# Feed-forward products on unnormed x: the inverse norm moves behind the matmuls

## The reference

```python
def rms_norm(x, w, eps=NORM_EPS):
    y = x32 * lax.rsqrt(jnp.mean(x32 * x32, axis=-1, keepdims=True) + eps)
    return (y * w.astype(F32)).astype(x.dtype)

def swiglu(x, w_gate, w_up, w_down):
    return (jax.nn.silu(x @ w_gate) * (x @ w_up)) @ w_down
# per layer:
x = x + 0.5 * swiglu(rms_norm(x, ffn1_norm), ...)      # hidden width 2816
x = x + hybrid_mixer(rms_norm(x, mix_norm), ...)
x = x + 0.5 * swiglu(rms_norm(x, ffn2_norm), ...)
```

## Time and profile before

| | |
|---|---|
| median of 3 runs | 1400.5 us (1397.87 to 1402.68) |
| the profiled execution | 1402.49 us |
| its span, first to last instruction | 1400.6 us |
| granted TensorE clock, mean | 0.985 |
| TensorE busy | 1348.2 us, 96% |
| VectorE busy | 925.3 us, 66% |
| ScalarE busy | 652.9 us, 47% |
| GpSimd busy | 350.9 us, 25% |

### The profile page before, as it was taken

One profiled execution on the slowest core, in us unless ns is written; L12 is line 12 of the kernel. 1 busy time (PEld: TensorE's weight loads), 2 busy tenths in 40 slices (PEclk: granted clock), 3 DMA queues, 4 the chain that ended last, 5 costly groups with the idle time before them and its releaser, 6 DMA issues.

```text
span 1400.6 us, 26198 instructions
## 1 busy us (share of the span) xinstructions
PE 1348.2 (96%) x11102; PEld 1312.7 (94%) x11102; DVE 925.3 (66%) x1323; ACT 652.9 (47%) x942; POOL 350.9 (25%) x235
## 2 busy tenths in 40 slices
PE   6999999999999999999999999998999999999998
PEld 6999999889898999999999999998888989999997
DVE  6777556876976865555477774567678677655554
ACT  6444547542234454444454454566322343544442
POOL 2000015445742720000210000244368245200000
PEclk9999999989999999999999999999899999999999
DMA  6565654533232646556556556464333335555553
GB/s 226 190 189 194 195 176 138 156 114 107 75 105 77 181 143 189 187 192 218 178 161 181 184 186 199 139 179 139 106 91 90 94 119 166 165 181 187 191 177 123
DMA packets 61316, 220.17 MB, mean 157 GB/s; under 512 B 6928, under 2 KB 7184, under 8 KB 60688
## 3 DMA queue, kind: packets, MB, share of 16 engines
q1 hardware_dynamic: 61200, 218.50, 49.6%
HBM read 217.42 MB, written 1.05 MB: 156 GB/s over the span
## 4 chain that ended last, share of the span: by engine, by line
PE 76%; DVE 16%; ACT 4%; issue 2%; DMA 1%; POOL 1%; SPq 0%; DVEq 0%; ACTq 0%
PE bank L480 23%; PE bank L481 22%; PE bank L482 22%; DVE wlo L1236 2%; PE bank L729 2%; DVE qkv L1451 2%; ACT whi L891 1%; PE bank L500 1%; DVE bank L1574 1%; DVE tmpA L1573 1%; DVE flat L1256 1%; PE bank L717 1%; DMA raw<-weights 1%; POOL wlo L1145 1%; DVE tmpA L1466 1%
## 5 line engine op out<-in xcount | busy, mean ns | idle before, releaser
L480 PE MATMUL bank<-xh,whi 128*128 128x256 f32 x2384 | 679.2, 285 | 7.0 <-DVE wlo L1236 3.0
L481 PE MATMUL bank<-xl,whi 128*128 128x256 f32 x2384 | 671.0, 281 | 0.0
L482 PE MATMUL bank<-xh,wlo 128*128 128x256 f32 x2384 | 669.5, 281 | 0.0
L1236 DVE TENSOR_TENSOR wlo<-raw,whi 128x1024 fp32r<-128x1024 f32 (+1 forms) x346 | 437.3, 1291 | 158.1 <-ACT whi L891 156.1
L480 PEld LDWEIGHTS bank<-xh,whi 128*128 128x128 f32 x2384 | 453.5, 190 | 16.4 <-issue 7.0
L891 ACT ACTIVATE whi<-raw 128x1024 fp32r<-128x1024 f32 (+1 forms) x414 | 417.7, 1035 | 99.4 <-DMA raw<-weights 78.6
L481 PEld LDWEIGHTS bank<-xl,whi 128*128 128x128 f32 x2384 | 453.5, 190 | 0.3
L482 PEld LDWEIGHTS bank<-xh,wlo 128*128 128x128 f32 x2384 | 453.1, 190 | 0.0
L1145 POOL TENSOR_TENSOR wlo<-raw,whi 128x1024 fp32r<-128x1024 f32 x68 | 172.4, 2542 | 204.2 <-ACT whi L891 204.2
L1186 POOL TENSOR_TENSOR flat<-flat 128x256 f32<-128x256 f32 x36 | 33.6, 933 | 716.3 <-ACT flat L910 715.3
L480 PE MATMUL bank<-hh,whi 128*128 128x256 f32 x704 | 196.9, 280 | 0.0
(11 more groups left out here) (347 smaller groups left out, 1409.6 us busy)
## 6 DMA issues: line engine op xcount, KB each, us to landing
raw<-weights SPq DMA_DIRECT2D x350, 512.0 KB, 3.8
raw<-weights SPq DMA_DIRECT2D x64, 448.0 KB, 4.0
cst<-consts SPq DMA_DIRECT2D x1, 1088.0 KB, 11.7
par<-params SPq DMA_DIRECT2D x1, 1072.5 KB, 7.9
par<-params SPq DMA_DIRECT2D x1, 1060.5 KB, 9.6
x<-x_in SPq DMA_DIRECT2D x1, 1024.0 KB, 6.1
y_out<-ret SPq DMA_DIRECT2D x4, 256.0 KB, 2.2
ropec<-positions SPq DMA_DIRECT2D x1, 128.0 KB, 2.1
```

What stands on the lines that cost most here:

```text
L480: mm(out, w[0], a[0], start=start, stop=False)
L481: mm(out, w[0], a[1], start=False, stop=False)
L482: return mm(out, w[1], a[0], start=False, stop=stop)
L1236: V.tensor_tensor(slot(wlo, i), slot(raw, i), r32(slot(whi, i)), ALU.subtract).then_inc(S("low_dve"), 1)
```

## The change

- For both feed-forward steps `xh` and `xl` are made from x times the norm weights, without the inverse norm: `high_scaled` on ScalarE and `low_scaled` on VectorE (all eight tiles; GpSimd makes none). At FFN2 and at FFN1 of layer 1 this is done tile by tile as the stage before hands x over.
- The sums of squares, and the matmuls that spread the inverse norm, now stand between the products of units 0 and 1 (`late_sums` before tile 4 of the gate halves, `late_inverse` before the first up half; in layer 0 `column_sums` and `late_inverse` within the up halves). Their `keep_busy` matmuls go. ScalarE copies the inverse norm to SBUF (`copy_inverse`).
- For every unit VectorE multiplies the gate by the inverse norm out of PSUM into `tmpB`, and ScalarE takes the SiLU from there. `up` runs one unit behind for the product with up and two for `hl`. In `down` of a feed-forward step there are two linked VectorE instructions: PSUM times factor times inverse norm, then the addition to x.
- At the start the first two weight pieces are transferred ahead of x, which comes in two halves; the large part of the parameters goes behind piece 7 and the large part of the constants behind piece 12. TensorE runs 24 `keep_busy` matmuls.
- The rotary remainders move from before layer 0 to between the last table step and `down` of layer 0. Units 0 and 1 now run before the S5 parameters, and table steps start with unit 11, so that the last two stand behind the last unit.
- The merged branches get `mgh` and `mgl` of their own, since `xh` and `xl` are filled while the output projection runs. The mixer's norm stays as it was. Of the feed-forward pieces `gu1_0.0` goes from GpSimd to VectorE.

```diff
         def sync_first(sp):
-            sp.dma_start(ropec.bitcast(mybir.dt.int32), positions).then_inc(once["small_loads"], 16)
             sp.dma_start(cst[:, 0:EARLY], consts[:, 0:EARLY]).then_inc(once["small_loads"], 16)
-            sp.dma_start(x, x_in).then_inc(once["x_load"], 16)
+            sp.dma_start(slot(raw, 0), weight_piece(0)).then_inc(once["raw0"], 16)
             sp.dma_start(par[:, 0:NORMS], layer_params(0)[:, 0:NORMS]).then_inc(S("norms"), 16)
-            for i in range(RAW_SLOTS):
-                sp.dma_start(slot(raw, i), weight_piece(i)).then_inc(once[f"raw{i}"], 16)
-            sp.dma_start(par[:, NORMS:], layer_params(0)[:, NORMS:]).then_inc(S("par"), 16)
-            sp.dma_start(cst[:, EARLY:], consts[:, EARLY:]).then_inc(once["tables_load"], 16)
+            sp.dma_start(slot(raw, 1), weight_piece(1)).then_inc(once["raw1"], 16)
+            sp.dma_start(x[:, 0:4, :], x_in[:, 0:4, :]).then_inc(once["x_load"], 16)
+            sp.dma_start(x[:, 4:8, :], x_in[:, 4:8, :]).then_inc(once["x_load2"], 16)
+            sp.dma_start(slot(raw, 2), weight_piece(2)).then_inc(once["raw2"], 16)
+            sp.dma_start(ropec.bitcast(mybir.dt.int32), positions).then_inc(once["position_load"], 16)
...
+                if i == 7:
+                    sp.dma_start(par[:, NORMS:], layer_params(0)[:, NORMS:]).then_inc(S("par"), 16)
...
+            def late_sums(which):
+
+                sum_of_first(which)
+                pe.wait_ge(*since("squares", 5 * which + 5))
+                for j in range(2):
+                    last = mm(sum_banks[j][:, 0:1], squared[:, KD - 1, j * P:(j + 1) * P], one_col, start=False, stop=True)
...
+                if f == 2:
+                    first_two(units, scaled, 0, early={4: lambda: late_sums(1)}, mid={0: lambda: late_inverse(2)})
...
+                    first_two(units, scaled, 0, mid={4: column_sums}, late={2: lambda: late_inverse(1)})
...
+            def high_scaled(wname, ks):
+
+                for k in ks:
+                    A(xh[:, k, :], x[:, k, :], ACT.Identity, scale=par_(wname, k, k + 1)).then_inc(S("xh"), 1)
...
-                    act.wait_ge(S("main"), main.ready(f"gu{f}_{m}"))
-                    if m >= 2:
-                        act.wait_ge(S("main_dve"), main.taken(f"gu{f}_{m - 2}"))
-                    A(tmpB[:, m % 2, :], main.bank(f"gu{f}_{m}")[:, 0:SEQ], ACT.Silu).then_inc(S(f"silu{f}"), 1)
+                    act.wait_ge(*since("gated", MF * (f - 1) + m + 1))
+                    A(tmpB[:, m % 2, :], tmpB[:, m % 2, :], ACT.Silu).then_inc(S(f"silu{f}"), 1)
...
+            copy_inverse(1)
+            silus(1, range(0, 2))
             act.wait_ge(S("par"), 16)
...
+                    if m == 0:
+                        dve.wait_ge(*since("inv_copied", f))
+                    dve.wait_ge(S("main"), main.ready(f"gu{f}_{m}"))
+                    V.tensor_tensor(tmpB[:, m % 2, :], main.bank(f"gu{f}_{m}")[:, 0:SEQ], invb, ALU.mult).then_inc(S("gated"), 1)
+                    if m:
+                        hidden(f, m - 1)
                     if m >= 2:
...
+                        low_hidden(f, m - 2)
...
+                            link(V.scalar_tensor_tensor(ps, ps, scale, over(invb, n), ALU.mult, ALU.mult))
+                            V.tensor_tensor(x[:, tiles, :], x[:, tiles, :], ps, ALU.add).then_inc(S("main_dve"), 1)
+                        if low and (done := tiles.start):
+                            low(range(done - (1 if done == 7 else 2), done))
...
+            up(1, [0, 1])
...
-            for m in range(9, MF):
+            for m in range(11, MF):
                 up(1, [m])
-                turn_tables(m - 9)
+                turn_tables(m - 11)
+            turn_tables(11)
+            if not Now.layer:
+                rope_turns()
             down("dn1_", 0.5)
```

More of the change, by code:

```diff
@@ L276, in trunk @@
         small = sb("small", 176)
+        invb = two("invb", 1)[:, 0, :]
+        mgh, mgl = (two(f"mg{part}", KD, dt=F32R, over="big", skip=8 * SEQ * i) for i, part in ((1, "h"), (2, "l")))
         ropec, ropes = two("ropec", 1)[:, 0, :], two("ropes", 1)[:, 0, :]
@@ L529, in half @@
                 wh, wl = piece(f"{unit}.{o}")
+                if unit.startswith("wo"):
+                    high, low = mgh, mgl
+                else:
+                    high, low = xh, xl
                 for k in range(KD):
-                    last = product(ps, (wh[:, k, :], wl[:, k, :]), (xh[:, k, :], xl[:, k, :]), k == 0, k == KD - 1)
+                    if k in at:
+                        at[k]()
+                    last = product(ps, (wh[:, k, :], wl[:, k, :]), (high[:, k, :], low[:, k, :]), k == 0, k == KD - 1)
                 last.then_inc(S("main" if PIECES[PIECE_INDEX[f"{unit}.{o}"]][2] else "part"), 1)
@@ L537, in pair, with column_sums, late_inverse, norm_tile @@
                 half(unit, 1)
-            def norm_tile(which, k):
-                return since("normed_pool" if k % 2 else "normed_dve", which * KD // 2 + k // 2 + 1)
-            def first_two(units, arrived, wait, bank=4):
+            def column_sums():
+                pe.wait_ge(once["squares_added"], 1)
+                for j in range(2):
+                    for k in range(4):
+                        last = mm(sum_banks[j][:, 0:1], squared[:, k, j * P:(j + 1) * P], one_col, start=(k == 0), stop=(k == 3))
+                last.then_inc(once["sums_in"], 1)
+            def late_sums(which):
+                sum_of_first(which)
+                pe.wait_ge(*since("squares", 5 * which + 5))
+                for j in range(2):
+                    last = mm(sum_banks[j][:, 0:1], squared[:, KD - 1, j * P:(j + 1) * P], one_col, start=False, stop=True)
+                last.then_inc(S("sums"), 1)
+            def late_inverse(f):
+                if f == 2:
+                    pe.wait_ge(*since("inv_rms", 2))
+                elif Now.layer:
+                    pe.wait_ge(*since("inv_rms", 0))
+                else:
+                    pe.wait_ge(once["inv_in"], 1)
+                for j in range(2):
+                    last = mm(inv_bank[:, j * P:(j + 1) * P], inv_rms[:, j:j + 1].to_broadcast([P, P]), ident, start=True, stop=True)
+                last.then_inc(once["inverse"], 1)
+            def norm_tile(k):
+                return since("normed_pool" if k % 2 else "normed_dve", k // 2 + 1)
+            def first_two(units, arrived, wait, bank=4, early={}, mid={}, late={}):
+                high, low = (mgh, mgl) if units[0] == "wo0" else (xh, xl)
                 banks = [main_bank(u) for u in units]
@@ L1292, in down @@
                         dve.wait_ge(S("main"), main.ready(unit))
[L1293 to L1301 removed]
+                        ps = halves(main.bank(unit)[:, 0:n * SEQ], n)
@@ L1303, in vector_layer @@
+            if not Now.layer:
+                split_to(2)
+                dve.wait_ge(S("norms"), 16)
+                dve.wait_ge(once["x_load"], 16)
+                dve.wait_ge(once["x_load2"], 16)
+                dve.wait_ge(once["small_loads"], 16)
+                low_scaled(1, "n1", range(KD))
+                split_to(4)
+                dve.wait_ge(once["rms_in"], 1)
+                V.reciprocal(inv_rms, rms_col).then_inc(once["inv_in"], 1)
+            up(1, [0, 1])
             lre, lim = par_("lre"), par_("lim")
```

262 lines of the change are left out of this document (136 added, 126 removed).

## The result

The changed kernel takes 1406.42 us in the median of 18 runs (1398.15 to 1411.23), the kernel before 1400.2 us (18 runs, 1397.72 to 1404.71). The ratio is 1.0048 with a 95% interval of 1.0035 to 1.006: slower by about 6.7 us by the ratio. Predicted were 1405.3 us and a range of 1395 to 1412. The profiled execution took 1408.41 us, span 1406.6, mean granted clock 0.979; before it was 1402.49, 1400.6 and 0.985.

The account below looks back on a forecast made before the run. TensorE, busy for all but 0.3 us of some 187 us in each feed-forward stage, was taken as the bound. Terms -9.45 +1.45 +0.95 +5.25 -0.3 +5.55 -5.7 -0.95 +1.35 +3.4 +3.3 = +4.85 gave 1405.3 us, range 1395 to 1412.

Parts of the forecast that it names:

- The start: Before the first product: it comes at 10.2 us instead of 19.65, 9.45 us earlier (9.0 to 10.5).
- Norm products: Units 0 and 1 of layer 0: TensorE pays for column sums (0.9) and inverse (0.55) between products, +1.45 us.
- Parameters: Layer 0, before piece 6: parameters queued behind piece 7 land at 30.5 us, piece ready 34.7, wanted 29.45; +5.25 us.
- The clock: Half clock after waits: +3.4 us for layer 0's two long stalls, +3.3 for two of four gaps of about 2 us.
- The second feed-forward part: Edge from output projection to FFN2: products start 4.25 us earlier, less 0.85 and 0.55; -2.85 us each, -5.7 for both.
- Layer 1's first feed-forward part: FFN1 of layer 1: products start 5.0 us earlier, partly given back by sums, inverse and a late piece 6; net -0.95 us.
- Units inside a stage: Steady units: VectorE's extra product of 0.42 us is covered by idle time, 0; units over 5.65 us would refute the prediction.
- Rival 5: VectorE becomes the bound of each unit: 1420 us or more; chance 0.03.
- rival 3: Splits are further ahead than read, so neither long stall of layer 0 arises: 1391 us, clearly faster; chance 0.14.
- rival 1: Parameters land by 28 us, the stall is 2.7 us without a clock fall: 1401.1 us, no change; chance 0.16.
- Rival 2: No gap lowers the clock: -6.7 us, 1398.6 us, still no change; chance 0.13.
- rival 4: All gaps lower the clock and the parameters take 7.9 us: 1411 us; chance 0.12.

Follow-up runs that it names:

- the early transfer: Changed kernel with the large parameter transfer issued at the very start, behind the positions, rather than behind weight piece 7; ratio 1.0037 to the kernel before.
- putting the pieces first: Changed kernel with weight pieces 6 and 7 split on ScalarE and VectorE ahead of the wait for the parameters; ratio 1.0006 to the kernel before.
- The spread chain: Changed kernel with the nine groups of rotary remainders run one behind each of the last nine units of layer 0's first feed-forward part; ratio 1.0009 to the kernel before.
- the filled waits: Changed kernel with 16 and 22 small products on constants ahead of the two long-stalled products, layer 0 only; ratio 1.001 to the kernel before.
- The second edge experiment: Changed kernel with both first pieces of the second feed-forward part split ahead of the third output-projection unit's scaled copies and square; ratio 1.0009 to the kernel before.
- the first edge experiment: Changed kernel with each output-projection weight piece split one piece earlier on ScalarE and VectorE, ahead of the scaled copies of x; ratio 1.0053 to the kernel before.
- the last kernel: Changed kernel with spread rotary steps, pieces ahead of parameters, both edge pieces split earlier, parameters issued early, ninth piece split between small-step groups; 1386.02 us, ratio 0.9906.

## Why the prediction came out as it did

The forecast (1405.3) is 1.1 us from the median, its sign and its mechanism were right: large gains at the edges, given back by low weight parts that come late in the order of VectorE's and ScalarE's queues. But several terms were off and cancelled, so that it came this close is in part luck.

**The start.** -8.84 for -9.45. I had x landed at 9.7; ScalarE began to scale its first half at 8.84, but VectorE, whose program waits for both halves, made the first low part at 10.19, and the first product followed 0.62 later. In the other executions with this start the first product was at 11.02 to 11.74, so this one was early.

**Norm products.** +1.45 predicted. The column sums took 1.70 us from the first of them to the next product (17.89 to 19.59) rather than 0.9, the inverse 0.36 rather than 0.55. The row that I costed them from gives records, and a float32 product on one column leaves two: x16 in the fence stands for 8 matmuls, and the earlier trace rows's x4 for two, not four. The column sums were 0.8 us too small, the whole term 0.6. Of the +0.95 for the pieces behind them, 0.58 came (a wait at 25.06).

**Parameters.** +5.25, measured 3.70. They were issued at 25.41, not 24.1, but landed after 5.8 us at 31.2 where I took 6.4 and 30.5. The path behind them was shorter than I had it: the scan took 0.69, not the 1.22 of the earlier trace rows, and the low part began 2.4 us after the landing. So the piece was ready at 34.8, and I had said 34.7. What was off is when TensorE wants it: it got there at 31.1, not at 29.45. Of these 1.7 us the start and the norm products make 0.6 each. That the landing alone is not the cause was shown by the early transfer, which left 2.95 of the 3.70 us; that the order of the queue is, by putting the pieces first (5.9 us).

**Rotary and tables.** +5.55, measured 5.14. The spread chain shows that it is the place in the queue that costs.

**Tails.** +1.35, measured +1.3: from the last down product to what follows it 0.46, 0.46 and 0.41 us more.

**The clock.** +3.4 for the two long waits, measured 4.7 by counting products (2.6 and 2.1), and 5.3, uncertain by 3, by filling them. I took the length of the half-clock stretch from the earlier trace rows, 3 us of products; here it was 5.7 and 4.4 us of products. For four gaps of about 2 us I added +3.3, and none of those lowered the clock in the changed kernel: 2.29 and 2.33 us at 1.00 after them. Together 4.7 for 6.7, and wrong in both parts. The Trainium skill, "TensorE: Matmul & The Clock Gate", HAM oscillation, describes that a wait between groups of matmuls puts the array back to half clock and that the next group then starts cold; this case agrees, with waits of 3.70 and 5.14 us, and it is what the filled waits took away.

**The second feed-forward part.** -5.7 for both layers, measured about -2.5 (from +8.7 to +7.4 and from +5.2 to +4.1, start of the output projection to the fourth unit). This is the largest miss, and here a step of the prediction was wrong. It said that TensorE "needs only the two pieces whose low parts VectorE makes at 509.21", with 0.35 us for one more scaling on ScalarE. The edge itself came near that: the next product followed the projection's last after 2.45 us in layer 0 where I had 2.0. What I had put at nothing is the projection ahead of it. Every output-projection unit puts two scaled copies, which wait for the new x, and a square ahead of the next high part on ScalarE (0.91 and 0.62 us at 509.87 and 510.69), an eviction and two low copies ahead of the low parts on VectorE. So the third output piece was late (1.00 us of waiting), and TensorE came to the edge 1.3 and 1.2 us later than it would have; VectorE stood idle for 1.66 us until that high part was there, so this one is ScalarE's queue. The second edge experiment shows that by order alone some 5.5 us more were to be had. The first one took 0.7 us of waits away in each layer and gave nothing in time: after its waits of 2.60 and 2.61 us the clock fell.

**Layer 1's first feed-forward part.** -0.95, measured about -2.0: from +7.4 at the start of the down product before it to +4.3 at the fourth unit, and 1.1 us of waits in its own down product. Its wait for piece 6 was 1.6 us, not 2.3.

**The sum.** With 1.0 for the pace of the products, the terms as measured add to +4.8; the profiled executions differ by 6.0. The missing 1.2 us are not assigned.

**Units inside a stage.** 0: with VectorE's further product of 0.42 in them, the units took 5.653 us in three stages and 5.600 in one, and in the kernel before the same two values stand in two stages each. So the term was right; the mark of 5.65 that I had set for being wrong lies inside this difference of pace and says nothing. Rival 5 is out, and so is rival 3, since both long waits were there, and rival 1, since the parameters took 5.8 us and landed at 31.2. Rival 2 is half true, and rival 4 out: the short gaps cost no clock here, the long waits did.

All the late parts are one mechanism: what makes the operand stands behind other work in a queue that runs in order. The Trainium skill, "TensorE: Matmul & The Clock Gate", Architectural detail, calls the queues of ScalarE and VectorE strictly first in, first out. The traces agree: VectorE stood for 2.52 us before the scan, and once the piece's split stands ahead of that wait, it is done on time.

## What to carry to other kernels

When a change moves the start of a stage forward, check at each edge which instruction makes the last operand ready and what stands ahead of it in its engine's queue; a block of small steps, a wait for a transfer or a copy that waits for its own input in front of it is paid as soon as the slack is used up. A wait of TensorE has a second price, the clock: here the two longest cost 2.6 and 2.1 us on top, those of 2.3 us mostly nothing, and filler matmuls in a wait that can't be removed buy it back. A change that measures slower may hold a faster kernel: here 4.8 of 1000 slower became 9 of 1000 faster by order alone.

## What the runs showed that was not expected

**The pace of products has two values at the same granted clock.** Within the changed kernel, 14 units of the first feed-forward part took 79.15 us in layer 0 and 78.40 in layer 1, 5.653 and 5.600 us each, both at granted clock 1.00. VectorE's first product of the sixth and the twentieth unit:

```profile
54.61 0.43 DVE L1318 TENSOR_TENSOR tmpB<-bank,invb 128x256 f32<-128x256 f32 x1 [0.97 <-PE bank L437]
...
133.76 0.42 DVE L1318 TENSOR_TENSOR tmpB<-bank,invb 128x256 f32<-128x256 f32 x1 [0.95 <-PE bank L437]
...
747.62 0.42 DVE L1318 TENSOR_TENSOR tmpB<-bank,invb 128x256 f32<-128x256 f32 x1 [0.91 <-PE bank L437]
...
826.02 0.42 DVE L1318 TENSOR_TENSOR tmpB<-bank,invb 128x256 f32<-128x256 f32 x1 [0.93 <-PE bank L437]
```

In the kernel before it was the other way round in these two stages. The last three stages of all fourteen profiled executions have one of the two values, 78.4 (34 times) or 79.15 us (8 times), and nothing between. A stage of some 187 us thus varies by up to 1.8 us, without a cause that the trace shows; part of the spread of 1398 to 1411 us may be this.

**Where the clock fell and where it didn't.** At the edges of the stages and in the first feed-forward part, waits of 2.15 and 2.29 us left it at 1.00, and so did twelve of 2.33 to 2.35 us in seven traces; waits of 2.60, 2.61, 2.95, 3.03, 3.70 and 5.14 us were followed by 0.50 to 0.59. The length alone does not decide. In the kernel with filled waits, TensorE waited 2.34 us at 1204.44, at the edge where the changed kernel's 2.33 us cost nothing, and here the clock fell:

```profile
1204.50:1207.50 3.00, 3.00 (x14) 0.50 0.82 300
```

Elsewhere in the traces it goes further apart: a wait of 3.57 us inside the mixer (the first edge experiment, at 952.32) left it at 1.00, and so did 2.50 us at 1141.42 in the last kernel. The length of the slow stretch varies too: after the wait of 3.69 us with the rotary chain spread it was 3.4 us, after the same wait of 3.70 us in the changed kernel 5.7. What one fall costs, some 1.5 to 2.6 us, is thus partly chance.

**Slow products where the window says 1.00.** Without the small products at the start, the first products follow each other after 0.213 us although the window has 1.00:

```profile
10.00:14.00 4.00, 2.19 (x10) 2.22 (x11) 3.47 (x9) 4.00 (x10) 0.00 (x0) 1.00 0.96 365
```

```profile
12.38 0.41 PE L437 MATMUL bank<-xh,wlo 128*128 128x256 f32 x1
12.59 0.41 PE L435 MATMUL bank<-xh,whi 128*128 128x256 f32 x1
```

The trace has no record of the clock before 14.95 us, which is also where the products become fast, and a window prints 1.00 where there is no record. At the start of an execution the distance between products is to be trusted, not the window's clock.
